# Attention's decay products ahead of the second head's projections, side blocks spread otherwise, RWKV state scaled behind the level mask

## The chip, the cores and the metric

One core of one Trainium2 chip runs the whole program. The metric is device time in microseconds (us) of one execution. The kernel before was run three times: 3910.09 us median, 3908.43 to 3912.69.

## The reference, cut to what matters

Two blocks over 512 tokens of width 1024, each of two layers, in float32. Block 1 per layer: modulated RMS norm, an RWKV-7 recurrence (8 heads of 64), a multiscale pooling, gates, output projection, gated feed-forward. Block 2 per layer: RMS norm, gated linear attention (GLA, 4 heads, key 128, value 256, both directions), grouped-query attention with rotary positions (8 heads), gates, feed-forward, and a gated per-layer embedding. What the change touches:

```python
# RWKV-7, per step
sk = einsum('bhvk,bhk->bhv', state, kk_t)
state = state * w_t - sk * (a_t * kk_t) + v_t * k_t
y_t = einsum('bhvk,bhk->bhv', state, r_t)
# GLA, per direction and head
la = log_sigmoid(ra @ w_alpha_up + b_alpha) / 16
cum = cumsum(la)                      # inside a chunk
q_dec, k_intra = q * exp(cum), k * exp(-cum)
# end of a layer of block 2
h = h + rms_norm(sigmoid(h @ w_ple_gate) * e, g_ple_post)
```

## The kernel before, in words

Five instruction streams are written out by hand and joined by semaphores: tensor, scalar, vector, gpsimd, sync. Activations lie feature-major, 128 features on the partitions and 512 tokens along the free axis. For float32 accuracy each operand is split into a high part (the round float32 format of the fast matmul) and a remainder, so each 128x128 weight block costs three matmuls of 512 columns (L420 to L422; L492 to L494 in side blocks; L815 to L817 in token-major products, where a product is 256 wide and each 128-token tile takes 24 of them).

Weights come as a stream of chunks of four blocks (256 KB), in exactly the order in which TensorE uses them, into a ring of 8 slots. The sync queue (SP) loads a chunk when TensorE has left the slot's last one (L2269); GpSimd makes the high part (L2245) and the remainder (L2247). The same queue carries the modulation columns (`ada_col`, 512 KB each, ring of three, L2263); the place of each is fixed by a list of chunk counts (`ada_at`), and a load is issued when the stream is 9 chunks past the place of the column three before it.

PSUM has 8 banks, dealt out in rotation by pool: "lin" banks 0 to 2, "lin2" 0 and 1, "bg2" 2 and 3, "bg" 3, "aux" 4 to 7. `begin` waits until the bank's last user has been read. `lane[0]` says which pool the projections take.

Where TensorE would wait for the other engines, it does side blocks: `side_jobs` names projections whose results are wanted only later (pool input and branch gates in block 1, 160 blocks a layer; one gate in each half of block 2, 64 blocks), and `fill(n)` does the next n of their blocks. ScalarE copies each finished gate to a staging tile and sends it to memory (`spill`, L1120 and L1123, in `gates_before`, with a wait for the spill before), and brings it back later (L1130, L1137). The constants at L57 to L63 say how many blocks stand where:

- `FILL_PREP` ahead of the RWKV chunks, `FILL_SCORE` behind each of the four score pairs of a chunk, `FILL_MEAN` (one number a layer) between mean and variance of each of four tiles, `FILL_POOL` ahead of the pool products; what is left is done behind the pool products, ahead of proj_a and proj_b.
- `FILL_CORE` ahead of each GLA head's core (four heads); inside a core 6 and 2 more; what is left is done behind head 3, ahead of the w_o_gla projections.

RWKV, `wkv_chunk`, four chunks of 128 tokens a layer: TensorE makes the scores of a pair of heads (L572, two banks) four times; VectorE multiplies each with the masks into `units` (L1861), then makes `mt` (L1866 twice, L1868); ScalarE copies the diagonal blocks into `ac`. TensorE starts the inversion (L586) when `mt` is there. VectorE makes the level masks 1 and 2 (L1873, in `level_part`), then goes through five levels with TensorE (L599, L611, L618; L1886), with one modulation column a level from the second on (L1666). Then w0, u, state and y. At the end of a chunk VectorE adds to the state `st` (L1903) and scales it (L1910); w0 and y of the next chunk read it.

GLA, `block2`: `group` makes ra, gq and gk of head 0; `gla_in` makes a head's gq, gk (for h > 0), values gv (token-major) and gates gg; `gla_decay` makes the decay logits of one head (two matmuls, L841), ScalarE takes Abs, Exp and Ln of them (L1368, L1372, L1375, two table loads), VectorE the sums (L1943 to L1966). Before, the order on TensorE is: decay 0, gv 0, decay 1, gg 0, gq 1, gk 1, decay 2, gv 1, decay 3, gg 1, core 0. `gla_factors` (ScalarE, L1386 to L1390) of head 0 waits for the sums of all four decays; `gla_keys` (VectorE, L1980 and L1983) makes qd and kd from them, for which the core's transposes (L853) wait. The core goes on with scores (L860), states (L870, L872), outputs (L884 to L888) and a norm (L895, L896); VectorE ends a head with `ot` (L2039, L2043) and its split into go_hi and go_lo (L1595, L1597), which the w_o_gla projections read.

The last norm of a block-2 layer: ScalarE squares the gated tiles (`square_gated`, L1439), TensorE sums them (L514), ScalarE takes the root (L1060).

## Time and profile before

| | |
|---|---|
| median of 3 runs | 3910.09 us |
| profiled execution, its own time | 3911.07 us |
| its span (first to last instruction) | 3909.2 us |
| mean granted TensorE clock | 0.975 |
| TensorE busy | 3731.4 us, 21300 matmuls |
| VectorE busy | 1806.1 us |
| ScalarE busy | 851.7 us |
| GpSimd busy | 2274.0 us |
| weight chunks | 1082, 256 KB each |

The profile is of one execution. Busy times of the engines overlap; the span is the time from the first to the last instruction, and the execution's own time is 1.9 us longer. A wait of an engine is idle time ahead of an instruction, put down to what ended it. Matmul durations in the timeline (0.39 us) are from start to end and overlap; the pace is read from the starts.

### The profile page before, as it was taken

The page shows a single profiled execution, that of the slowest core. Times are in us where ns is not written, and L with a number is a line of the kernel's source. Part 1 is how long each engine was busy: PE and PEld are TensorE (multiplying, and loading weights), DVE is VectorE, ACT ScalarE, POOL GpSimd, SP SyncE. Part 2 cuts the span into 40 slices and gives each one's busy share as a digit, 9 for nine tenths or more (in the row PEclk, how much of TensorE's full clock was granted, in tenths as well). Part 3 has the DMA queues.
Part 4 walks back from the last instruction along what each step waited for, and adds up shares of the span by engine and source line. Part 5 has one row for each costly group of instructions (what it writes and reads, how often), then busy time and mean ns, then how long its engine had stood idle before and what let it go on. Part 6 is the DMA issues. An engine that isn't in the chain of part 4 may idle for free.

```text
span 3909.2 us, 52952 instructions
## 1 busy us (share of the span) xinstructions
PE 3731.4 (95%) x21300; PEld 3022.7 (77%) x21300; DVE 1806.1 (46%) x2338; ACT 851.7 (22%) x1334; POOL 2274.0 (58%) x2218
## 2 busy tenths in 40 slices
PE   5999999999999899999899999999989999999997
PEld 4777678887777678887788677888777876778886
DVE  5643754234744653124443654523454435553235
ACT  3322110004222110003321532000243225220002
POOL 4512768776512767774556356777645463567773
PEclk9999999999999999998999999999989999999999
DMA  4223444342223443332223133333312231323332
GB/s 184 87 83 103 138 143 146 113 151 77 75 82 99 137 146 108 97 97 66 75 73 122 52 102 82 97 97 96 98 50 79 86 103 55 110 82 97 97 97 68
DMA packets 192195, 386.08 MB, mean 99 GB/s; under 512 B 21456, under 2 KB 21584, under 8 KB 190288
## 3 DMA queue, kind: packets, MB, share of 16 engines
q1 hardware_dynamic: 169776, 338.24, 29.1%
q10 hardware_dynamic: 22176, 44.45, 3.2%
q8 instruction: 170, 2.79, 0.3%
q14 instruction: 73, 0.60, 0.0%
HBM read 361.64 MB, written 20.97 MB: 98 GB/s over the span
## 4 chain that ended last, share of the span: by engine, by line
PE 86%; DVE 8%; ACT 4%; DMA 1%; issue 1%; ACTq 0%; SPq 0%; DVEq 0%
PE psum L420 18%; PE psum L421 18%; PE psum L422 18%; PE psum L492 3%; PE psum L494 3%; PE psum L493 3%; PE psum L514 2%; PE psum L981 1%; PE psum L956 1%; PE psum L599 1%; PE psum L611 1%; PE psum L467 1%; PE psum L468 1%; PE psum L469 1%; PE psum L618 1%; PE psum L572 1%
## 5 line engine op out<-in xcount | busy, mean ns | idle before, releaser
L2245 POOL TENSOR_SCALAR w_hi<-raw 128x512 fp32r<-128x512 f32 x1082 | 747.3, 691 | 1493.2 <-DMA raw<-weight_chunks 1489.5
L2247 POOL TENSOR_TENSOR w_lo<-raw,w_hi 128x512 fp32r<-128x512 f32 x1082 | 1491.1, 1378 | 90.3
L420 PE MATMUL psum<-in_hi,w_hi 128*128 128x512 f32 x1920 | 761.6, 397 | 3.8 <-ACT hs L1325 1.3
L421 PE MATMUL psum<-in_lo,w_hi 128*128 128x512 f32 x1920 | 749.3, 390 | 0.0
L422 PE MATMUL psum<-in_hi,w_lo 128*128 128x512 f32 x1920 | 748.8, 390 | 0.0
L420 PEld LDWEIGHTS psum<-in_hi,w_hi 128*128 128x128 f32 x1920 | 361.8, 188 | 91.7 <-issue 11.1
L421 PEld LDWEIGHTS psum<-in_lo,w_hi 128*128 128x128 f32 x1920 | 361.7, 188 | 79.8 <-issue 6.2
L422 PEld LDWEIGHTS psum<-in_hi,w_lo 128*128 128x128 f32 x1920 | 361.6, 188 | 75.7
L492 PE MATMUL psum<-in_hi,w_hi 128*128 128x512 f32 x576 | 255.0, 443 | 0.0
L494 PE MATMUL psum<-in_hi,w_lo 128*128 128x512 f32 x576 | 226.5, 393 | 0.0
L493 PE MATMUL psum<-in_lo,w_hi 128*128 128x512 f32 x576 | 226.4, 393 | 0.0
L1841 DVE TENSOR_TENSOR hs<-hs,psum 128x512 f32<-128x512 f32 x44 | 30.2, 687 | 295.5 <-PE psum L422 281.8
L2177 DVE TENSOR_TENSOR hs<-psum,rs_t 128x512 f32<-128x512 f32 x88 | 60.9, 691 | 228.5 <-PE psum L422 227.8
L1325 ACT ACTIVATE hs<-psum 128x512 f32<-128x512 f32 x44 | 26.3, 598 | 531.9 <-PE psum L422 531.8
L1666 DVE SCALAR_TENSOR_TENSOR ada_col<-ada_col,c_act 128x1024 f32<-128x1024 f32 x80 | 115.9, 1449 | 55.1 <-DMA ada_col<-ada_slabs 52.6
L492 PEld LDWEIGHTS psum<-in_hi,w_hi 128*128 128x128 f32 x576 | 108.6, 188 | 38.8 <-issue 17.3
L420 PE MATMUL psum<-hid_hi,w_hi 128*128 128x512 f32 x352 | 136.9, 389 | 0.0
L421 PE MATMUL psum<-hid_lo,w_hi 128*128 128x512 f32 x352 | 136.9, 389 | 0.0
L422 PE MATMUL psum<-hid_hi,w_lo 128*128 128x512 f32 x352 | 136.9, 389 | 0.0
L420 PE MATMUL psum<-h_hi,w_hi 128*128 128x512 f32 x352 | 136.9, 389 | 0.0
L421 PE MATMUL psum<-h_lo,w_hi 128*128 128x512 f32 x352 | 136.9, 389 | 0.0
L422 PE MATMUL psum<-h_hi,w_lo 128*128 128x512 f32 x352 | 136.9, 389 | 0.0
(427 smaller groups left out, 6700.4 us busy)
## 6 DMA issues: line engine op xcount, KB each, us to landing
raw<-weight_chunks SPq DMA_DIRECT2D x1082, 256.0 KB, 2.6
ada_col<-ada_slabs SPq DMA_DIRECT2D x80, 512.0 KB, 4.3
spill<-gate_st ACTq DMA_DIRECT2D x56, 256.0 KB, 2.7
ada_at<-ada_slabs SPq DMA_DIRECT2D x8, 1024.0 KB, 15.6
gin<-spill ACTq DMA_DIRECT2D x32, 256.0 KB, 3.4
mgs<-spill ACTq DMA_DIRECT2D x32, 256.0 KB, 3.0
sml<-small ACTq DMA_DIRECT2D x4, 1024.0 KB, 5.2
spill<-nt ACTq DMA_DIRECT2D x16, 256.0 KB, 2.6
```

The source lines that it names most:

```text
L420: pe.matmul(bank[:], wh, hi[:, i, :], start=(i == 0), stop=False)
L421: pe.matmul(bank[:], wh, lo[:, i, :], start=False, stop=False)
L422: ins = pe.matmul(bank[:], wl, hi[:, i, :], start=False, stop=(i == len(blocks) - 1))
L467: pe.matmul(bank[:], wh, in_hi[:, k, :], start=(k == 0), stop=False)
L492: pe.matmul(bank[:], wh, in_hi[:, k, :], start=(k == 0), stop=False)
L493: pe.matmul(bank[:], wh, in_lo[:, k, :], start=False, stop=False)
L494: ins = pe.matmul(bank[:], wl, in_hi[:, k, :], start=False, stop=(k == DT - 1))
L514: ins = pe.matmul(bank[:, t:t + 1], src[:, t * P:(t + 1) * P], kst[:, K_ONES, 0:1], start=(first and t == 0), stop=last, skip_group_check= ...
L1666: ins = stt(buf[:], buf[:], 1.0, c_act[:], ALU.mult, ALU.mult, accum_out=mods[l][:, m:m + 1])
L2177: tt(h[:, i, :], bank_of(job)[:], rs_t[:], ALU.mult).then_inc(bank_read(job), 1)
L2245: ts(w_hi[:, slot, :], raw[:, slot, :], 1.0, 1.0, ALU.mult, ALU.mult).then_inc(sem("chunk_hi"), 1)
L2247: ins = tt(w_lo[:, slot, :], raw[:, slot, :], w_hi[:, slot, :].bitcast(F32), ALU.subtract)
```

## The change

Five edits. The counts of side blocks in three constants. On both TensorE and ScalarE, the decays of block 2: decay 2 goes from behind head 1's gq and gk to ahead of them, and decay 3 from behind head 1's values to ahead of them. The pool of banks "lin2" is entered behind the first two heads' inputs instead of ahead of them. On ScalarE, the last of eight squares goes ahead of the activation that loads the Sqrt table. On VectorE, the state is scaled in the next chunk, between the masks of levels 1 and 2, instead of at the end of the chunk.

```diff
--- before.py
+++ after.py
@@ -57,10 +57,10 @@
 FILL_PREP = (8, 24)
 PE_BEFORE_SUM = 2
 PE_BEFORE_SPREAD = 4
-FILL_SCORE = (0, 2, 2, 4)
-FILL_MEAN = (16, 12)
+FILL_SCORE = (0, 2, 0, 5)
+FILL_MEAN = (16, 13)
 FILL_POOL = 8
-FILL_CORE = (8, 2, 2, 8)
+FILL_CORE = (5, 2, 2, 15)
 
 
 WINDOW_CHUNK = (8, 8, 10, 12)
@@ -819,15 +819,15 @@
                     ins.then_inc(done_sem(name + (t,)), 1)
                     close(name + (t,))
 
-            def gla_in(l, h, h_in, decays=()):
+            def gla_in(l, h, h_in, first=None, second=None):
                 if h:
                     projection(("gq", l, h), "w_in2", l, N_GQ + h, h_in)
                     projection(("gk", l, h), "w_in2", l, N_GK + h, h_in)
-                for d in decays[:-1]:
-                    gla_decay(l, d)
+                if first is not None:
+                    gla_decay(l, first)
                 token_major(("gv", l, h), l, "w_in2", N_GV + 2 * h)
-                for d in decays[-1:]:
-                    gla_decay(l, d)
+                if second is not None:
+                    gla_decay(l, second)
                 for j in range(2):
                     projection(("gg", l, h, j), "w_in2", l, N_GG + 2 * h + j, h_in)
 
@@ -924,9 +924,10 @@
                 group([(("ra", l), "w_in2", l, N_RA), (("gq", l, 0), "w_in2", l, N_GQ),
                        (("gk", l, 0), "w_in2", l, N_GK)], h_in)
                 side_jobs([(("g2a", l, m), "w_in2", l, N_GA + m) for m in range(DT)], "bg2")
+                gla_in(l, 0, h_in, 0, 1)
+                gla_decay(l, 2)
+                gla_in(l, 1, h_in, 3)
                 lane[0] = "lin2"
-                gla_in(l, 0, h_in, (0, 1))
-                gla_in(l, 1, h_in, (2, 3))
                 for h in range(GH):
                     gla_core(l, h)
                     if h + 2 < GH:
@@ -1333,7 +1334,7 @@
             norm_root(("nf", 0))
             squares(("m1", 0), ("rs", ("nf", 0)))
 
-            def gla_in(l, h, decays=()):
+            def gla_in(l, h, first=None, second=None):
                 if h >= 2:
                     act.wait_ge(sem("qd_ready"), count("qd_ready", (l, h - 2)))
                 for job, dst in ((("gq", l, h), gq[h % 2]), (("gk", l, h), gk[h % 2])):
@@ -1341,16 +1342,16 @@
                     act.wait_ge(*done(job))
                     af(dst[:], bank_of(job)[:], ACT.Copy).then_inc(bank_read(job), 1)
                     act.wait_ge(bank_read(job), turn(job))
-                for d in decays[:-1]:
-                    gla_decay(l, d)
+                if first is not None:
+                    gla_decay(l, first)
                 for t in range(NCH):
                     job = ("gv", l, h, t)
                     gates_before(job, gate_st2)
                     act.wait_ge(*done(job))
                     af(gv[h % 2][:, t, :], bank_of(job)[:, 0:GDV], ACT.Copy).then_inc(bank_read(job), 1)
                     act.wait_ge(bank_read(job), turn(job))
-                for d in decays[-1:]:
-                    gla_decay(l, d)
+                if second is not None:
+                    gla_decay(l, second)
                 if h >= 2:
                     act.wait_ge(sem("split_ready"), count("split_ready", ("go", l, 2 * (h - 2) + 1)))
                 for j in range(2):
@@ -1446,8 +1447,9 @@
                 act.wait_ge(*done(job))
                 af(ra[:], bank_of(job)[:], ACT.Copy).then_inc(bank_read(job), 1)
                 act.wait_ge(bank_read(job), turn(job))
-                gla_in(l, 0, (0, 1))
-                gla_in(l, 1, (2, 3))
+                gla_in(l, 0, 0, 1)
+                gla_decay(l, 2)
+                gla_in(l, 1, 3)
                 gla_factors(l, 0)
                 for h in range(GH):
                     gla_core(l, h)
@@ -1559,9 +1561,9 @@
                     act.wait_ge(bank_read(job), turn(job))
                     if m:
                         square_gated(l, m - 1)
+                square_gated(l, DT - 1)
                 af(warm[:], eps[:, 2:3], ACT.Sqrt).then_inc(sem("scalar_step"), 1)
                 act.wait_ge(sem("scalar_step"), passed("scalar_step"))
-                square_gated(l, DT - 1)
                 norm_root(("m5", l))
                 if l == 0:
                     squares(("m1", 1))
@@ -1875,6 +1877,10 @@
 
                 dve.wait_ge(sem("diag_ready"), count("diag_ready", (l, c)))
                 level_part(1)
+                if c:
+                    ins = tt(st[:], st[:], sscal[:, :, c - 1:c].to_broadcast([P, RT, P]), ALU.mult)
+                    ins.then_inc(sem("state_ready"), 1)
+                    dve.wait_ge(sem("state_ready"), passed("state_ready", (l, c)))
                 level_part(2)
                 for v in range(1, len(LEVELS)):
                     for name, t, second in (("mam", mi, 0), ("mamt", mt, 1)):
@@ -1907,9 +1913,6 @@
                         else:
                             ins.then_inc(sem("vector_step"), 1)
                             dve.wait_ge(sem("vector_step"), passed("vector_step"))
-                    ins = tt(st[:], st[:], sscal[:, :, c:c + 1].to_broadcast([P, RT, P]), ALU.mult)
-                    ins.then_inc(sem("state_ready"), 1)
-                    dve.wait_ge(sem("state_ready"), passed("state_ready", (l, c + 1)))
 
             def four(k):
```

## Rows read from the trace of the kernel before

**Rows 1.** Page, part 1: busy us, share of the span, instructions
```profile
PE 3731.4 (95%) x21300; PEld 3022.7 (77%) x21300; DVE 1806.1 (46%) x2338; ACT 851.7 (22%) x1334; POOL 2274.0 (58%) x2218
```

**Rows 2.** TensorE's waits: line, releaser, us in total, times, longest
```profile
PE psum L853 <- DVE kd L1983: 19.1, 2, 9.5
PE psum L586 <- DVE mt L1868: 17.0, 8, 2.2
PE psum L860 <- DVE ot L2039: 6.7, 2, 3.3
PE psum L815 <- ACT gv L1350: 5.7, 4, 1.4
PE psum L508 <- DVE yt L1792: 4.1, 3, 1.7
PE psum L514 <- ACT sqd L1439: 2.2, 2, 1.1
```

**Rows 3.** Timeline, TensorE, first w_o_gla projection: start, us, engine, line, operation
```profile
2064.78 0.39 PE L420 MATMUL psum<-go_hi,w_hi 128*128 128x512 f32 x1
2069.54 0.39 PE L420 MATMUL psum<-go_hi,w_hi 128*128 128x512 f32 x1
```

**Rows 4.** Timeline, VectorE, third chunk of layer 0; in brackets idle before, releaser
```profile
278.02 1.42 DVE L1861 TENSOR_TENSOR units<-psum,kst 128x512 f32<-128x512 f32 x2 [0.88 <-PE psum L572]
281.22 1.64 DVE L1868 TENSOR_TENSOR mt<-kst,mt 128x512 f32<-128x512 f32 x1
290.27 0.69 DVE L1873 TENSOR_TENSOR bm<-ac,kst 128x512 f32<-128x512 f32 x1
```

**Rows 5.** Timeline, GpSimd, the same chunk
```profile
279.57 1.08 POOL L2245 TENSOR_SCALAR w_hi<-raw 128x512 fp32r<-128x512 f32 x1 [9.77 <-DMA raw<-weight_chunks]
```

**Rows 6.** Windows: us; busy of five engines; granted clock; DMA share; GB/s
```profile
2039.00:2045.00 6.00, 6.00 (x29) 5.50 (x29) 5.08 (x10) 0.00 (x0) 0.00 (x0) 0.72 0.01 3
3093.00:3099.00 6.00, 6.00 (x26) 5.51 (x26) 4.27 (x8) 0.00 (x0) 0.00 (x0) 0.60 0.00 0
178.75:181.75 3.00, 3.00 (x37) 2.13 (x37) 1.65 (x2) 1.19 (x2) 2.21 (x2) 0.61 0.01 3
```

**Rows 7.** Timeline, VectorE, end of the same chunk
```profile
313.52 1.78 DVE L1666 SCALAR_TENSOR_TENSOR ada_col<-ada_col,c_act 128x1024 f32<-128x1024 f32 x1 [6.64 <-DMA ada_col<-ada_slabs]
322.50 0.88 DVE L1903 TENSOR_TENSOR st<-psum,st 64x256 f32<-64x256 f32 x2 [7.18 <-PE psum L690]
```

**Rows 8.** Page, part 6: DMA issues, KB each, median us to landing
```profile
spill<-gate_st ACTq DMA_DIRECT2D x56, 256.0 KB, 2.7
```

**Rows 9.** Timeline, ScalarE, linear attention of layer 0
```profile
1890.27 0.60 ACT L1360 ACTIVATE sg<-psum 128x512 f32<-128x512 f32 x1 [2.43 <-PE psum L422]
1896.62 1.28 ACT L1386 ACT_TABLE_LOAD   x1 [5.75 <-DVE dsc L1966]
```

**Rows 10.** Timeline, VectorE, the same stretch
```profile
1865.50 1.54 DVE L1943 TENSOR_SCALAR la<-psum,col 128x512 f32<-128x512 f32 x2 [6.55 <-ACT ln L1368]
1876.85 0.16 DVE L1966 TENSOR_TENSOR dsc<-dsc,la 128x3 f32<-128x3 f32 x1
1896.38 0.16 DVE L1966 TENSOR_TENSOR dsc<-dsc,la 128x3 f32<-128x3 f32 x1
1903.46 1.63 DVE L1983 TENSOR_TENSOR kd<-gk,ln 128x512 f32<-128x512 f32 x1
```

**Rows 11.** Timeline, VectorE, end of the fourth head
```profile
2067.38 1.66 DVE L1597 TENSOR_TENSOR go_lo<-ot,go_hi 128x512 fp32r<-128x512 f32 x1
```

**Rows 12.** Timeline, ScalarE, last norm of layer 1
```profile
3889.52 1.28 ACT L1562 ACT_TABLE_LOAD   x1
3891.05 0.63 ACT L1439 ACTIVATE sqd<-yy 128x512 f32<-128x512 f32 x1
3892.88 0.26 ACT L1060 ACTIVATE root<-psum,eps 128x4 f32<-128x4 f32 x1 [1.20 <-PE psum L514]
```

**Rows 13.** Timeline, VectorE, the same stretch
```profile
3888.94 0.69 DVE L2200 TENSOR_TENSOR yy<-mg,ee 128x512 f32<-128x512 f32 x1 [4.02 <-ACT mg L1558]
```

## The prediction

> **What bounds the kernel now.** The page's first part comes first: TensorE (PE) is busy 95% of the span [rows 1], so all that can be won without removing products is the 178 us in which it idles, plus what it loses at a lower clock. The list of PE's waits says where: 19.1 us before the transposes of the first attention head, 17.0 us before each chunk's inversion in the RWKV stage, 6.7 us before the scores of the fourth head, 5.7 us in the token-major value products, 4.1 us in the mean/variance stage of layer 1, 2.2 us before the last token sums [rows 2]. Each is short and repeated, so I go to the timeline around one of each and ask what ends it. The change touches six places; nearly everything in it is a move. A side block is three matmuls, started 0.68 us apart: eight blocks of one projection start between 2064.78 and 2069.54, seven steps in 4.76 us [rows 3]. The number of side blocks is fixed, so a block taken from one place is paid at another, and only idle time counts.
>
> **RWKV chunks (8).** Before: after scores d=2 PE does two side blocks, then scores d=3, then four. VectorE (DVE) sits idle 0.88 us before the last two mask products because of those two blocks (1.1 to 1.3 in the other seven chunks); the three steps behind them end with L1868, 1.64 us long, and only then may PE start the inversion [rows 4]. After: the two blocks go, so scores d=3 come 1.37 us earlier and the last pair of products follows the pair before it directly: 1.2 us earlier. PE has one block fewer to hide the rest (-0.68). That alone is 0.5 us a chunk. The larger part is L1868: an equal product from SBUF, L1873, takes 0.69 us when GpSimd (POOL) is idle [rows 4], and POOL's weight split began at 279.57, in the middle of this chain [rows 5]. The split comes 2.7 us after four blocks are used up, which now is 20 blocks = exactly five weight chunks per RWKV chunk, so it hits the same spot eight times. With 19 blocks the fourth one falls into the fill behind the scores, and the phase moves by one from chunk to chunk: I work out the split just behind L1868 in the first two chunks, on part of L1866 in the third, on L1868 in the fourth. Per layer the gain in idle is 1.5+1.7+1.2+0.6, in all about 9.5 us. Bounds: -5.5 us (nothing earlier, eight blocks less cover), 4.2 us (earlier scores only), 14.2 us (no split in any chain). PE's clock: after such a wait the granted clock is 0.61 over 3 us [rows 6], the 1.2 GHz level for most of it; 4 of the 8 stretches show a drop (0.61, 0.70, 0.75, 0.77), 1.2 to 1.6 us each. With waits of under 1 us most go: +4 us (0 to 6).
>
> **State scaled later** (L1910): DVE's 0.69 us leaves the head of the chain, but the scores of d=2 come behind PE's two blocks either way, so DVE only waits longer. Cost and gain 0; in its new place it delays the mask of level 2 by 0.7 us, which is used some 6 us later. If the cover went, 0.7 us a chunk.
>
> **The modulation products** hang on the same blocks: SP issues their load when the 16th block is done, DVE takes it at 313.52, and the state add comes at 322.50 [rows 7], 7.2 us of room behind it. With 19 blocks the release moves behind the cross and w0 steps, some 4 us: room 3 us, about 1 in the first chunk of a layer. I take 0.
>
> **Mean stage, layer 1:** +1 block in each of four turns. Three turns wait for yt, 4.1 us in all [rows 2], so three of the four blocks are covered: +2.0. Layer 0 keeps 16, so its four blocks fall behind the pool products. There they delay the last gate: its copy (0.60) and spill (2.7 us to land [rows 8]) now stand ahead of the gate loads on ScalarE's (ACT's) queue, and the whole proj_a/proj_b stretch follows those loads. 3.3 us later, 2.7 of it work: -0.6.
>
> **Linear attention (2 layers).** (a) Three banks in place of two for the first two heads: the third token tile needn't wait for ACT's copy of the first, which stands behind decay work. All 5.7 us [rows 2] go. (b) Head 0. Before: last gate copy ends 1890.87, but factors start at 1896.62, because [rows 9] the fourth decay's sums only end at 1896.54; keys ready 1905.09 [rows 10]. After: the third decay moves ahead of the second head's projections and the fourth ahead of the values. A decay beside values takes DVE 11.5 us, 1865.50 to 1877.01 [rows 10], and the fourth is then done near 1878. So the wait for the sums is gone, and the last gate copy is next: it comes 2.9 us earlier by (a), at 1888.0. Factors and keys take 8.5 us (1896.62 to 1905.09): ready at 1896.5. PE reaches the fill at 1887.3, waits 0.8 us for bank 2 (by the count of rotations the last gate product now lies in the side blocks' first bank, in both layers; hidden by the wait behind it), does 5 blocks (3.4), and waits to 1896.5: idle 5.8 instead of 9.5, +3.7 a layer, 7.4. Bounds 4 (keys slower by 1.7) and 12 (POOL quiet at the keys). (c) Head 3 gets 7 more blocks, 4.8 us, ahead of a wait of 3.3 a layer: +6.7, and the granted clock of 0.72 and 0.60 over 6 us behind it [rows 6] recovers: +1.7 and +2.4. (d) The price: 8 blocks instead of 12 remain between head 3 and w_o_gla, 2.7 us less. There the eighth block starts at 2069.54 [rows 3], and its input is ready at 2069.04 [rows 11]: 0.5 us of room. New wait 2.2 us a layer, and one of the two clocks drops: -5.6 (bounds -3 and -9). Moved instructions: two products per decay, and ACT's chain of six activations and two table loads, 6.8 us; the copies of gq and gk queue behind it, which PE doesn't wait for with three banks. Side blocks finish elsewhere, so gate copies (0.6 and a spill issue) shift on ACT; each falls where ACT waits for PE. Cost 0; if not, 0.9 us each.
>
> **Last square** ahead of the Sqrt table load, twice. ACT loads the table at 3889.52 and squares at 3891.05, root at 3892.88 [rows 12]; the input was ready at 3889.63 [rows 13]. After: square 3889.7, table and warm-up from 3890.35 to 3891.9 beside PE's sums (1.1 us), root at 3891.9: +1.0 each, 1.9. A rule speaks against it: the Trainium skill, ScalarE: Activation LUTs, section What ACT_TABLE_LOAD costs, gives 1283 ns for the load and 1380 ns of drain. The rows agree with the load's length and leave no room for the rest: load and warm-up together take 1.53 us, 3889.52 to 3891.05 [rows 12]. By the page's sum root would be later than now, 0.3 us each instead of 1.0 earlier.
>
> **Sum:** 9.5 + 4 + 2.0 - 0.6 + 5.7 + 7.4 + 6.7 + 4.1 - 5.6 + 1.9 = 35.1 us. From the profiled execution's own 3911.07 us (1 us over the median 3910.09): 3876.
>
> **Rivals.**
> 1. POOL's splits stay on the masks: the shift of one block moves them by 0.7 us or a fill, and products of 0.7 to 1.6 us are easily hit. Then the chunks give 4.2 and no clock: 35.1 - 9.3 = 25.8, 3885. The Trainium skill, SBUF — State Buffer, section Who interferes with whom, says such a DVE product is blocked for the rest of POOL's instruction; by that rule, [rows 4, 5] agree (1.64 against 0.69 us).
> 2. Attention gives back more: the longer fill of head 3 keeps POOL busy beside DVE's ot chain (1.5 us of wait left a layer, clock low again, -7), and (d) costs 3 more. 3886; with rival 1, 3895.
> 3. Slower: the modulation load. If the block that frees it falls behind the 19th, into the next chunk's first fill, DVE waits for it in front of the state add, and the masks behind that: release near 273.3, 5 us of load, 1.8 of product, 280.2 against a state add at 270.6, 9.6 us at each of six transitions, 58 us: 3876 + 58 = 3934. Against: my count gives blocks 16 and 17 in the phases that matter, inside the chunk.
> 4. It doesn't do what it says: only one decay really moves ahead of the projections, and if the factors are held by the gate copies as much as by the sums, while masks come no sooner (-5.5), gains and prices cancel: 3905 to 3910.
> 5. The table switch costs the page's drain: 3878.5.
>
> **Chances.** Forecast 0.60 (its own range 3866 to 3885), rival 1 0.20, rival 2 with or without 1 0.10, rival 5 0.02: all faster, 0.92. Rival 4: 0.03, taken as no change. Rival 3: 0.05. A measurement of this kernel tells about 0.2%, 8 us, from no change. The range 3861 to 3896: below, chunks at 14.2 and 6, head 0 at 12; above, rivals 1 and 2 together.
>
> **What would show it.** Waits of PE: kd near 10 us and a bank wait of 0.8 ahead of the fill, mt L1868's group (now line +4 or so) from 17 to under 9, ot and gv gone, yt near 2, a new wait for go_lo near 4.4; L1868's product near 0.7 us in about half the chunks; root 1 us sooner behind the last square. Wrong if the mt wait stays over 2 us a chunk, if kd stays over 15, or if the state add waits for an ada load.

## The result, and the profile after

The kernel after takes 3861.65 us (median of 4 runs, 3860.92 to 3868.89), the kernel before 3909.53 us beside it: ratio of after to before 0.9881, 95% interval 0.9868 to 0.9895, 47.9 us less. Forecast were 35.1 us less, 3876 us, with a range from 3861 to 3896: the right direction, but the median lies only 0.65 us above the lower edge of the range. The profiled execution of the kernel after is the slowest of its four, 3868.89 us, so that profile against profile the gain is 42.2 us.

The page of the kernel after, part 1 (busy us, share of the span, instructions), answers to [rows 1]:

```profile
PE 3717.1 (96%) x21300; PEld 3015.2 (78%) x21300; DVE 1797.5 (46%) x2338; ACT 851.8 (22%) x1334; POOL 2274.2 (59%) x2222
```

With the same 21300 matmuls TensorE is busy 14.3 us less and idle 27.9 us less (149.9 in place of 177.8): part of the gain is not idle time but TensorE's clock. TensorE's waits (line, releaser, us in total, times, longest) answer to [rows 2], and like them they are an excerpt; L586 waits for L1870 now, the old L1868:

```profile
PE psum L853 <- DVE kd L1986: 9.1, 2, 4.6
PE psum L586 <- DVE mt L1870: 8.4, 8, 1.7
PE psum L420 <- DVE go_lo L1599: 4.6, 2, 3.0
PE psum L508 <- DVE yt L1794: 1.8, 2, 1.1
PE psum L492 <- ACT sg L1361: 1.5, 2, 0.7
PE psum L514 <- ACT sqd L1440: 0.8, 1, 0.8
```

The waits for ot and gv are gone, kd and mt are halved, and two waits are new, go_lo and the bank held by sg. Forecast were 10, under 9, 4.4, near 2 and 1.6 for the first five. One longer wait is in neither excerpt, that of L420 for mt (L1818, behind proj_a and proj_b): 15.4 us before, 13.6 after, and between 10.3 and 15.4 in the fourteen profiles of this study.

**The masks of a chunk.** VectorE in the first and the third chunk of layer 0 (start, us, engine, line, operation), against [rows 4]:

```profile
174.61 1.41 DVE L1868 TENSOR_TENSOR mt<-units,kst 64x512 f32<-64x512 f32 x2
176.05 0.69 DVE L1870 TENSOR_TENSOR mt<-kst,mt 128x512 f32<-128x512 f32 x1
...
270.53 2.17 DVE L1868 TENSOR_TENSOR mt<-units,kst 64x512 f32<-64x512 f32 x2
272.74 0.69 DVE L1870 TENSOR_TENSOR mt<-kst,mt 128x512 f32<-128x512 f32 x1
```

GpSimd's split in the same two chunks, against [rows 5]:

```profile
176.65 0.62 POOL L2248 TENSOR_SCALAR w_hi<-raw 128x512 fp32r<-128x512 f32 x1 [4.61 <-DMA raw<-weight_chunks]
...
269.45 0.62 POOL L2248 TENSOR_SCALAR w_hi<-raw 128x512 fp32r<-128x512 f32 x1 [10.81 <-DMA raw<-weight_chunks]
```

In the first chunk the split starts 0.6 us after the last product began, and that product takes 0.69 us in place of 1.64. In the third it has moved forward onto the pair before it (2.17 in place of 1.41). The phase drifts as the prediction worked out, and PE's waits for mt follow it: 0.80, 0.80, 1.56, 1.15 in layer 0 and 0.79, 0.81, 1.66, 0.81 in layer 1, against 2.1 eight times before.

**The clock behind these waits.** Windows of 8 us that take in the wait or its end, second chunk of layer 0 (us; busy of five engines; granted clock; DMA share; GB/s), first before, then after:

```profile
228.00:236.00 8.00, 6.57 (x89) 5.13 (x89) 2.95 (x3) 1.20 (x2) 2.95 (x3) 0.79 0.13 35
```

```profile
220.00:228.00 8.00, 7.20 (x86) 5.37 (x87) 6.42 (x8) 3.06 (x5) 3.16 (x3) 1.00 0.18 66
```

Four of the eight chunks of before show 0.79 in such a window; none of after does. 0.21 of 8 us is 1.7 us each. The prediction had read it over 3 us only [rows 6] and so missed the rest of each spell at the 1.2 GHz level.

Another drop got longer. Layer 1's first scores stand behind a wait for bonus (L1783), 2.59 us before and 3.38 after, and at the start of that chunk (6 us, first before, then after) the clock reads:

```profile
1047.00:1053.00 6.00, 6.00 (x31) 4.39 (x31) 4.02 (x6) 1.20 (x2) 1.88 (x2) 0.77 0.33 124
```

```profile
1037.00:1043.00 6.00, 5.61 (x21) 4.25 (x22) 4.39 (x7) 1.20 (x2) 1.60 (x2) 0.50 0.27 101
```

From its first pair of scores to its third that chunk takes 1.3 us longer for it than before (6.14 against 4.88).

**Head 0**, layer 0, against [rows 9, 10]. ScalarE's last gate copy and the table load of the factors:

```profile
1868.86 0.60 ACT L1361 ACTIVATE sg<-psum 128x512 f32<-128x512 f32 x1 [3.56 <-PE psum L422]
1869.47 1.28 ACT L1387 ACT_TABLE_LOAD   x1
```

VectorE's last keys:

```profile
1876.13 1.63 DVE L1986 TENSOR_TENSOR kd<-gk,ln 128x512 f32<-128x512 f32 x1
```

TensorE's fill and the transposes behind it:

```profile
1869.51 0.50 PE L492 MATMUL psum<-in_hi,w_hi 128*128 128x512 f32 x1 [0.75 <-ACT sg L1361]
1877.82 1.54 PE L853 MATMUL psum<-kst,kd 128*128 128x128 f32 x6 [4.62 <-DVE kd L1986]
```

The table load of the factors follows the last gate copy directly; before, 5.75 us of waiting for the sums lay between. From its start to the end of the keys it is 8.3 us (forecast 8.5), and the bank wait is 0.75 (forecast 0.8).

**Last norm, layer 1**, ScalarE, against [rows 12]:

```profile
3848.84 0.63 ACT L1440 ACTIVATE sqd<-yy 128x512 f32<-128x512 f32 x1 [0.21 <-DVE yy L2203]
3849.49 1.28 ACT L1565 ACT_TABLE_LOAD   x1
3851.02 0.26 ACT L1061 ACTIVATE root<-psum,eps 128x4 f32<-128x4 f32 x1
```

The first token sum starts at 3847.09, root 3.93 us behind it; before, 4.92 (3887.96 to 3892.88). That is the 1.0 us forecast.

**The modulation load** (rival 3). VectorE at the change to the second chunk of layer 1, against [rows 7]:

```profile
1084.48 1.63 DVE L1668 SCALAR_TENSOR_TENSOR ada_col<-ada_col,c_act 128x1024 f32<-128x1024 f32 x1 [10.35 <-DMA ada_col<-ada_slabs]
...
1086.54 0.88 DVE L1909 TENSOR_TENSOR st<-psum,st 64x256 f32<-64x256 f32 x2 [0.42 <-PE psum L690]
```

The product now waits for its load until close ahead of the state add, but the add still waits for TensorE, not for the load. Of the room, 5.20 us at this change before, 0.42 us is left; at the later changes it is 2.8 and 12.3 us. In e6 to e9, e11 and e13 below nothing is left at the first change of layer 1, in some of them of layer 0 too: the add follows the product at once, and in e7 TensorE then waits 0.22 and 0.73 us for the state. So rival 3 does exist, on a small scale.

### The profile page after: what moved, and what is told of

It reads as the page before. It is cut to its first block, busy times and chain, and to the rows that moved or that the text cites. A ratio compares the mean times of both kernels' runs of the same rounds, so it can differ in the third digit from the quotient of the medians.

```text
span 3867.0 us, 52950 instructions
## 1 busy us (share of the span) xinstructions
PE 3717.1 (96%) x21300; PEld 3015.2 (78%) x21300; DVE 1797.5 (46%) x2338; ACT 851.8 (22%) x1334; POOL 2274.2 (59%) x2222
## 4 chain that ended last, share of the span: by engine, by line
PE 86%; DVE 9%; ACT 2%; DMA 1%; issue 1%; ACTq 0%; SPq 0%; DVEq 0%
PE psum L420 18%; PE psum L421 18%; PE psum L422 18%; PE psum L492 3%; PE psum L494 2%; PE psum L493 2%; PE psum L514 2%; PE psum L982 1%; PE psum L957 1%; PE psum L611 1%; PE psum L467 1%; PE psum L599 1%; PE psum L815 1%; PE psum L817 1%; PE psum L816 1%; PE psum L468 1%
## 5 line engine op out<-in xcount | busy, mean ns | idle before, releaser
L420 PE MATMUL psum<-in_hi,w_hi 128*128 128x512 f32 x1920 | 761.2, 396 | 2.9 <-ACT hs L1326 1.3
L420 PEld LDWEIGHTS psum<-in_hi,w_hi 128*128 128x128 f32 x1920 | 361.8, 188 | 90.7 <-issue 11.1
L1530 ACT ACTIVATE hs<-hs 128x512 f32<-128x512 f32 x44 | 27.8, 633 | 495.9 <-DVE hs L2180 495.9
L420 PE MATMUL psum<-hid_hi,w_hi 128*128 128x512 f32 x352 | 136.9, 389 | 0.0
L420 PE MATMUL psum<-h_hi,w_hi 128*128 128x512 f32 x352 | 136.9, 389 | 0.0
```

Of the source, the lines that this page charges most:

```text
L420: pe.matmul(bank[:], wh, hi[:, i, :], start=(i == 0), stop=False)
```

## The experiments

Experiments e1 to e4 take the change apart, each part alone on the kernel before (median beside them 3911.4 us of 19 runs). Theory A, of the prediction: waits and clock in the chunks, and waits in the linear attention, are two separate gains; the state's new place and the square are small. Its rivals were that the state's place carries the chunk gain, and that the parts share one gain.

**e1, blocks of the RWKV stage alone.**

```diff
-FILL_SCORE = (0, 2, 2, 4)
-FILL_MEAN = (16, 12)
+FILL_SCORE = (0, 2, 0, 5)
+FILL_MEAN = (16, 13)
```

> The kernel before with FILL_SCORE (0, 2, 0, 5) and FILL_MEAN (16, 13) alone. Theory A (scores come earlier, the weight split leaves the mask products, TensorE's clock no longer drops behind the chunk waits): 20 to 24 us faster than before; the eight mt waits fall from 17.0 to about 8.5 us in all and the granted clock in the 3 us behind each is 1.00. Theory B (the later state scaling carries part of it, because VectorE starts its masks 0.7 us sooner in six chunks): 14 to 19 us, mt waits of 10 us or more.

Measured: 3887.48 us, ratio 0.9939 (0.9922 to 0.9955), 23.9 us less. The wait for mt is 6.2 us, for kd 19.1 as before, and the clock over the 3 us behind each of the eight waits is 1.00. The constants carry the whole RWKV gain: the eight chunks take 391.0 us here, 393.2 in the kernel after and 416.2 before.

**e2, the state's place alone.**

```diff
                 level_part(1)
+                if c:
+                    ins = tt(st[:], st[:], sscal[:, :, c - 1:c].to_broadcast([P, RT, P]), ALU.mult)
...
-                    ins = tt(st[:], st[:], sscal[:, :, c:c + 1].to_broadcast([P, RT, P]), ALU.mult)
```

> The kernel before with the state scaled behind the mask of level 1 alone. Theory A: VectorE waits longer for the scores of d=2 and nothing else moves: within 1 us of before, mt waits 17 us. Theory B: 0.7 us at six chunk starts reach TensorE: 4 us faster, mt waits near 13 us.

Measured: 3909.56 us, ratio 0.9995 (0.9986 to 1.0004); mt 17.1. No effect that shows, as forecast.

**e3, linear attention alone** (on TensorE; ScalarE's order of the decays likewise).

```diff
-FILL_CORE = (8, 2, 2, 8)
+FILL_CORE = (5, 2, 2, 15)
...
+                gla_in(l, 0, h_in, 0, 1)
+                gla_decay(l, 2)
+                gla_in(l, 1, h_in, 3)
                 lane[0] = "lin2"
-                gla_in(l, 0, h_in, (0, 1))
-                gla_in(l, 1, h_in, (2, 3))
```

> The kernel before with the decay order, the banks and FILL_CORE (5, 2, 2, 15) of the changed kernel alone. Theory A: the linear attention stages are independent of the rest: 20 to 22 us faster, kd wait near 9 us, ot and gv waits gone, a new go_lo wait near 4.5 us. Theory B: part of what the attention stage showed came from the phase of the weight stream, shifted by the RWKV side blocks: 15 us or less.

Measured: 3889.33 us, ratio 0.9944 (0.9929 to 0.9959), 22.1 us less. kd 9.4, go_lo 5.6, sg 1.5; ot and gv gone; mt 17.2.

**e4, the last square alone.**

```diff
+                square_gated(l, DT - 1)
                 af(warm[:], eps[:, 2:3], ACT.Sqrt).then_inc(sem("scalar_step"), 1)
                 act.wait_ge(sem("scalar_step"), passed("scalar_step"))
-                square_gated(l, DT - 1)
```

> The kernel before with the last square ahead of the Sqrt table load alone. By the rows (load 1.28 us, next activation right behind it): 2 us faster, root 1.0 us sooner behind the start of the last token sums. By the page's drain: 0.6 us slower, root 0.3 us later.

Measured: 3908.85 us, ratio 1.0000 (0.9990 to 1.0009). The wait for sqd falls from 2.2 us to 0.8; in the time, where 2 us were expected, it is below what this measurement separates.

The product of the four ratios is 0.9878, the whole change has 0.9881: within their intervals the parts add up, and none hides another.

Experiments e5 to e8 vary the kernel after, one thing each (kernel before beside them: 3913.5 us).

**e5, twenty blocks a chunk; e6, nineteen but two of them ahead of scores d=3.** With before and after they make a table of order by count.

```diff
-FILL_SCORE = (0, 2, 0, 5)
-FILL_MEAN = (16, 13)
+FILL_SCORE = (0, 2, 0, 6)
+FILL_MEAN = (16, 12)
```

> The kernel after with FILL_SCORE (0,2,0,6) in place of (0,2,0,5) and FILL_MEAN (16,12) in place of (16,13): 20 side blocks a chunk again, but the scores of d=3 still without blocks ahead of them. Theory A (what counts is how late mt comes behind the scores, that is earlier scores plus POOL's split off the last product): five weight chunks a RWKV chunk put the split at the same spot eight times, the one it has in the first chunk of after, just behind the last mask product. One block more covers 0.68 us of the waits of 0.8 (and 1.6 in the third chunk goes to the same): the wait for mt falls from 8.4 us to under 2, eight times 0.1 to 0.2; the fill in the mean stage of layer 1 has one block fewer a turn, its wait for yt goes from 1.8 to about 4 us, and layer 0's left-over blocks behind the pool products vanish. In sum 4 to 6 us under the kernel after. Rival B (the phase must drift from chunk to chunk, or the split will lie on the masks, as in before): waits of 1.5 us a chunk, clock below 0.8 again behind them, 5 to 10 us over the kernel after.

```diff
-FILL_SCORE = (0, 2, 0, 5)
+FILL_SCORE = (0, 2, 2, 3)
```

> The kernel after with FILL_SCORE (0,2,2,3): the 19 blocks a chunk of after, but two of them still ahead of the scores of d=3. It tells the two halves of the chunk gain apart. Theory A1 (earlier scores carry it, POOL's phase is a side matter): waits for mt of 2.0 us or more in all eight chunks, as 1.2 us of VectorE's idle time returns, low clock behind about half of them, 15 to 20 us over the kernel after. Theory A2 (the split off the last product carries it): the split moves by one block a chunk, so two or three chunks of four have the last product at 0.7 us and waits near 1.8, the others over 2.8; 10 to 14 us over the kernel after.

Measured: e5 3862.02 us (3855.35 to 3867.77), ratio 0.9872 (0.9853 to 0.9891); e6 3882.15 us, ratio 0.9923 (0.9908 to 0.9937). PE's wait for mt, in us over eight chunks:

| | 20 blocks | 19 blocks |
|---|---|---|
| two blocks ahead of scores d=3 | 17.0 (before) | 16.8 (e6) |
| none ahead | 0 (e5) | 8.4 (after) |

e5 has no line for this wait at all; 0.1 us of idle time a chunk without a releaser stays. VectorE in its first chunk:

```profile
172.51 1.41 DVE L1868 TENSOR_TENSOR mt<-units,kst 64x512 f32<-64x512 f32 x2
173.95 0.69 DVE L1870 TENSOR_TENSOR mt<-kst,mt 128x512 f32<-128x512 f32 x1
174.67 2.71 DVE L1875 TENSOR_TENSOR bm<-ac,kst 128x512 f32<-128x512 f32 x2
```

GpSimd beside it:

```profile
174.54 0.62 POOL L2248 TENSOR_SCALAR w_hi<-raw 128x512 fp32r<-128x512 f32 x1 [4.96 <-DMA raw<-weight_chunks]
```

The split now starts 0.4 to 0.8 us after the product that TensorE waits for has begun, eight times out of eight; the product takes its 0.69 us, and the split falls on the level masks (2.71 us for two here), which nobody waits for. So the phase need not drift; it must only be the right one, and rival B falls. The table says more: with 20 blocks as before, moving the scores alone takes the whole wait away, and the count of 19 gives 8.4 us of it back. Yet eight blocks more in the chunks are 5.4 us of work for these 8.4 us, and the eight fronts (from the first score to the inversion) are only 1.9 us shorter than in after, 83.9 against 85.9. The rest of what was expected lay at the mean stage and behind the pool products. In the time, where 4 to 6 us less were expected, e5 can't be told from the kernel after.

In e6 the split moves through the chunks. VectorE in its second and fourth chunk of layer 0, where PE waits 1.55 and 2.53 us:

```profile
225.12 1.41 DVE L1868 TENSOR_TENSOR mt<-units,kst 64x512 f32<-64x512 f32 x2
226.56 0.69 DVE L1870 TENSOR_TENSOR mt<-kst,mt 128x512 f32<-128x512 f32 x1
...
326.60 2.36 DVE L1868 TENSOR_TENSOR mt<-units,kst 64x512 f32<-64x512 f32 x2
329.00 0.69 DVE L1870 TENSOR_TENSOR mt<-kst,mt 128x512 f32<-128x512 f32 x1
```

0.95 us more for the pair of products is 0.98 us of longer wait; in the first chunk of each layer it is the last product that is longer (1.64 us). Four of eight chunks wait 1.5 to 1.6 us, four 2.5 to 2.8: A2's pattern, and not A1's 2.0 or more in all eight. The time fits A1's 15 to 20 us better: 20.5 us over after by the medians (16 by the ratios), where A2 expected 10 to 14. Both halves count: the split's place moves a single wait by 1.0 us, but the sum over the eight, 16.8 us, is that of before, and it is the order that halves it. Of 15.3 us in the chunks of the two profiles, 12.6 are in the fronts (98.5 against 85.9), 2.7 behind them. The waits for mt make 8.4 of the 12.6; another part is the change between side blocks and scores itself. TensorE's last two pairs of scores in the third chunk of layer 0, before:

```profile
274.14 0.70 PE L572 MATMUL psum<-qr,b_f 64*128 64x256 f32 x4
274.67 0.60 PE L572 MATMUL psum<-qr,k_f 64*128 64x256 f32 x4
276.79 0.70 PE L572 MATMUL psum<-qr,b_f 64*128 64x256 f32 x4
```

And after:

```profile
266.40 0.70 PE L572 MATMUL psum<-qr,b_f 64*128 64x256 f32 x4
266.94 0.60 PE L572 MATMUL psum<-qr,k_f 64*128 64x256 f32 x4
267.37 0.60 PE L572 MATMUL psum<-qr,b_f 64*128 64x256 f32 x4
```

From pair to pair it is 2.65 us with the blocks and 0.97 without, 1.68 less, of which two blocks are 1.37: 0.31 us come on top of the work moved.

**e7, four blocks from heads 1 and 2 to head 0; e8, old order of the decays.**

```diff
-FILL_CORE = (5, 2, 2, 15)
+FILL_CORE = (9, 0, 0, 15)
```

> The kernel after with FILL_CORE (9,0,0,15): the two side blocks ahead of each of heads 1 and 2 go ahead of head 0, where TensorE still waits 4.6 us a layer for the keys. Theory: those four blocks hide nothing where they are (no wait stands there in after), and each hides 0.68 us in its new place: kd's wait falls from 9.1 to 3.7 us, 5.4 us under the kernel after. Rival: without them a wait appears at head 1 or 2 (qd or kd of these heads, or ot), which takes back 1 to 1.5 us at each of four places: no change.

```diff
                 gla_in(l, 0, h_in, 0, 1)
-                gla_decay(l, 2)
-                gla_in(l, 1, h_in, 3)
+                gla_in(l, 1, h_in, 2, 3)
```

(and the same on ScalarE)

> The kernel after with the order of the decays as before (0, values 0, 1, gates 0, gq 1, gk 1, 2, values 1, 3, gates 1), all else as after. Theory: the sums of the fourth decay end late again and hold ScalarE's factors; head 0 has now five blocks to cover it in place of eight, so kd's wait goes from 9.1 us to about 20: 9 to 13 us over the kernel after. Rival (the three banks alone free the chain, since the last gate copy comes as late as the sums): within 3 us of the kernel after.

Measured: e7 3850.10 us (3848.17 to 3851.79), ratio 0.9841 (0.9824 to 0.9857), 11.5 us under the kernel after (16 by the ratios); e8 3876.38 us, ratio 0.9909 (0.9894 to 0.9924), 14.7 over it (11 by the ratios; 9 to 13 expected). PE's waits of e7, then of e8:

```profile
PE psum L853 <- DVE kd L1986: 3.8, 2, 1.9
...
PE psum L420 <- DVE go_lo L1599: 1.0, 2, 0.5
```

```profile
PE psum L853 <- DVE kd L1984: 18.6, 2, 9.3
```

e8: without the new order the sums hold the factors again, and the wait for kd is as long as before. But the wait alone misleads, since TensorE reaches it at different times. Counted from the first decay product (L841) of layer 0, in us (layer 1 differs by some 0.2 at most):

| | last gate copy ends | last sums end | last kd ends | TensorE starts to wait |
|---|---|---|---|---|
| before (two banks, old order) | 64.93 | 70.61 | 79.16 | 69.68 |
| e8 (three banks, old order) | 61.56 | 67.22 | 74.53 | 65.31 |
| e9 (two banks, new order) | 64.90 | 53.61 | 73.25 | 67.61 |
| after (three banks, new order) | 61.55 | 52.08 | 69.86 | 65.30 |

So the third bank alone brings the keys 4.6 us forward and the new order another 4.7; the third bank's share doesn't show in the wait because TensorE comes 4.4 us earlier too (two of these for the three blocks fewer). Of the 4.6 us, 0.9 are one kd product that takes 0.69 us in e8 and 1.63 in before and after.

e7: kd is where it was expected (3.7), and no wait appears at heads 1 and 2. The surplus is the wait for go_lo, 4.6 to 1.0 us. It was not expected; VectorE's closing chain of head 3 in the kernel after, and in e7:

```profile
2034.03 1.40 DVE L1597 CAST go_hi<-ot 128x512 fp32r<-128x512 f32 x1
...
2036.98 1.58 DVE L2046 TENSOR_TENSOR ot<-ot,sg 128x512 f32<-128x512 f32 x1
...
2039.05 0.98 DVE L1599 TENSOR_TENSOR go_lo<-ot,go_hi 128x512 fp32r<-128x512 f32 x1
```

```profile
2023.45 0.43 DVE L1597 CAST go_hi<-ot 128x512 fp32r<-128x512 f32 x1
...
2025.71 0.88 DVE L2046 TENSOR_TENSOR ot<-ot,sg 128x512 f32<-128x512 f32 x1
...
2027.09 1.06 DVE L1599 TENSOR_TENSOR go_lo<-ot,go_hi 128x512 fp32r<-128x512 f32 x1
```

The same products, 10.9 us from reciprocal to end in one and 9.8 in the other; in layer 1 it is 12.2 and 9.9. These 1.1 and 2.4 us are nearly all of the 3.6 us of wait: GpSimd's splits again, in another phase. Behind the wait for kd the clock of 6 us is 0.72 and 1.00 in e7, where it is 0.60 and 0.56 in the kernel after: 3.4 us more.

**e9, two banks; e11, four blocks back behind head 3; e12 and e13, combinations** (kernel before beside these four: 3906.2 us, 7 us less than beside e5 to e8, so ratios say more than medians across the two groups).

```diff
+                lane[0] = "lin2"
                 gla_in(l, 0, h_in, 0, 1)
                 gla_decay(l, 2)
                 gla_in(l, 1, h_in, 3)
-                lane[0] = "lin2"
```

> The kernel after with the pool of banks lin2 entered ahead of the first two heads' inputs, as before; the decays stay in their new order. Theory: the values of heads 0 and 1 wait again for ScalarE's copy of the tile before the last, 5.7 us in the two layers as before, and the last gate copy comes 2.9 us later a layer; the wait of 1.5 us for a bank ahead of head 0 (copy of sg) goes. Since kd waits 9.1 us for a chain that starts at that copy, kd's wait shrinks by no more than what the values' waits push the fill back: time 4 to 8 us over the kernel after. Rival (the waits for gv went with the decays' order, not with the third bank): no wait for gv, within 2 us of the kernel after.

```diff
-FILL_CORE = (5, 2, 2, 15)
+FILL_CORE = (5, 2, 2, 11)
```

> The kernel after with FILL_CORE (5,2,2,11): four of the fifteen blocks ahead of head 3 stay for the place ahead of w_o_gla. It weighs the gain (c) against the price (d) of the prediction. Theory: 11 blocks cover three more than before's 8, 2.0 of the 3.3 us that head 3 waited for ot, so 1.3 us a layer return, 2.6 in all; the wait for go_lo, 4.6 us in the two layers, goes altogether: idle 2 us less than in after, and the clock decides: 0 to 4 us under the kernel after. Rival (the fill of 15 keeps GpSimd busy beside VectorE's ot, so fewer blocks make ot sooner): no wait for ot at all, 4 to 6 us under it.

```diff
-FILL_SCORE = (0, 2, 0, 5)
-FILL_MEAN = (16, 13)
-FILL_CORE = (5, 2, 2, 15)
+FILL_SCORE = (0, 2, 0, 6)
+FILL_MEAN = (16, 12)
+FILL_CORE = (9, 0, 0, 15)
```

> Two edits of earlier runs together: FILL_SCORE (0,2,0,6) with FILL_MEAN (16,12), and FILL_CORE (9,0,0,15). The second alone gave 3850.1 us, 11.5 under the kernel after; the first alone gave 3862.0, where its profile has no wait for mt at all, against 8.4 us, and where eight blocks more in the chunks (5.4 us) were saved at the mean stage and behind the pool products. Theory: the parts add up; the idle time worked out is 3 to 6 us less than with the second alone: 3844 to 3850. Rival (weight chunks in the same phase in every RWKV chunk cost elsewhere what the wait gives): 3850 to 3858.

```diff
-FILL_CORE = (5, 2, 2, 15)
+FILL_CORE = (9, 0, 0, 15)
...
                 level_part(1)
-                if c:
-                    ins = tt(st[:], st[:], sscal[:, :, c - 1:c].to_broadcast([P, RT, P]), ALU.mult)
...
+                    ins = tt(st[:], st[:], sscal[:, :, c:c + 1].to_broadcast([P, RT, P]), ALU.mult)
```

> FILL_CORE (9,0,0,15) as in e7, and the state scaled at the end of the chunk, as before. The first experiment (blocks alone, state at the end) showed 6.2 us of wait for mt in eight chunks, the kernel after 8.4 us. Theory (the state's place costs nothing): within 2 us of e7's 3850.1. Rival (its new place between the masks of the levels pushes mi and mt of the level steps, or moves weight chunks' phase, 0.3 us a chunk): 2 to 5 us under e7.

| | median us | ratio to before, 95% | wait kd | other waits, us |
|---|---|---|---|---|
| after | 3861.65 | 0.9868 to 0.9895 | 9.1 | mt 8.4, go_lo 4.6 |
| e9 | 3871.70 | 0.9902 to 0.9932 | 11.5 | gv 5.7, go_lo 4.5 |
| e11 | 3860.72 | 0.9871 to 0.9901 | 8.5 | ot 2.6, gs 1.6 |
| e7 | 3850.10 | 0.9824 to 0.9857 | 3.8 | mt 8.1, go_lo 1.0 |
| e12 | 3850.77 | 0.9841 to 0.9872 | 3.0 | yt 4.1, no mt |
| e13 | 3851.10 | 0.9846 to 0.9879 | 4.0 | mt 7.7 |

e9: 10 us over the kernel after (14 by the ratios), where 4 to 8 were expected. The 5.7 us for gv are back, and kd didn't shrink but grew by 2.4: the chain to the keys starts at the last gate copy, which two banks delay as well, by 3.4 us a layer. The third bank paid twice. In its profile the two attention stages are 6.2 us longer than in after, as expected; a stage that no edit touches (from layer 1's first norm sums, L514, to L508, ahead of its RWKV chunks) takes 101.6 against 95.5 us at a clock of 0.87 against 0.93, as it does in the profiles of e1 and e2, so part of the surplus may not be the edit's. e11: the trade of (c) and (d) comes out even in the time, 2.6 us of ot wait (as expected) against 4.6 of go_lo. e12: no mt wait, yet no gain over e7; in its profile TensorE idles 4.2 us less than in e7's (3850.0 - 3714.3 against 3849.9 - 3710.0) and is busy 4.3 us longer. The clock's scatter doesn't explain it: the mean granted clock is 0.980 in both. Whether it is a price of the constant phase, one profile of each doesn't tell; this stays open, and the time lies in the rival's range. e13: by the medians within 1 us of e7, as expected, by the ratios 9 us over it, with intervals that overlap: no worth of the state's place shows. e7, e12 and e13, 3850 to 3851 us, have lower medians than both kernels of the case; e7's interval alone lies wholly under that of the kernel after.

## Why the prediction was right, and where its sizes were off

Term by term, in the two profiled executions. For a chunk, "front" is from the first score to the start of the inversion, "rear" the rest; a minus is time saved.

| step of the prediction | forecast | measured |
|---|---|---|
| chunks, front: idle 9.5 and a block (0.68) fewer in each of eight | -14.9 | -16.5 |
| chunks, rear: clock | -4 | -6.5 |
| mean stage of layer 1: 4 blocks in, 2.0 covered | +0.7 | +0.5 |
| layer 0's left-over blocks | +3.3 | +2.4 |
| linear attention, both layers | -18.3 | -21.2 |
| last square | -1.9 | -1.0 in layer 1; -0.8 in layer 0, with a change of clock in it |

**Chunks.** The eight fronts sum to 102.4 us before and 85.9 after, the rears to 313.8 and 307.4. The rears hold the same work, and they differ by 1.6 us in exactly the four chunks whose window shows 0.79. What happens in the kernel after is as forecast: earlier scores, the split off the last product in most chunks, waits under 1 us in five of eight. Why it happens was half wrong. The prediction gave the scores' new place 4.2 us (its bound for "earlier scores only") and the larger part to the count of 19, which makes the phase drift. In e5, with 20 blocks and the new place alone, the split is off the product eight times out of eight and the wait is gone; in e6, with 19 and the old place, the wait is what it was. The order carries the gain, and the drift costs 8.4 us of it, for which the blocks taken out of the chunks pay back 5.4. That the sum came out near 9.5 is luck in this respect (and its four terms a layer, 1.5 + 1.7 + 1.2 + 0.6, make 10.0 in two layers).

In the front, 16.5 us are 8.6 of waits for mt (17.0 less 8.4; 9.5 forecast), 5.4 of blocks, and 2.5 that no step had: 0.4 to 0.6 us in each of seven chunks, the 0.31 us found with e6 among it, less 0.8 in the first chunk of layer 1, where the low clock behind the wait for bonus lasts longer. The step that was mis-sized most is "1.2 to 1.6 us each" for a spell of low clock: each is 1.7 us by windows of 8 us, four of them, 6.5 us against the 4 taken and the bound of 6. Rival 1 (splits stay on the masks) is refuted by the rows of both chunks above.

That such a product is held while GpSimd works agrees with the rule of the Trainium skill, SBUF — State Buffer, section Who interferes with whom, in the pairs here: 0.69 against 1.64, 0.43 against 1.40, 0.88 against 1.58 us (the 0.88 is itself held for a part; free it is 0.69). It holds the other way too. In the last chunk of layer 1 in the kernel after, the last product starts at 1195.58 and takes its 0.69 us; the split that starts just behind it is the longer one, 1.14 in place of 0.62 us:

```profile
1195.62 1.14 POOL L2248 TENSOR_SCALAR w_hi<-raw 128x512 fp32r<-128x512 f32 x1 [10.45 <-DMA raw<-weight_chunks]
```

**State scaled later: nothing that shows**, by e2 and e13.

**Attention.** (a) gv: all 5.7 us, as forecast, and e9 shows that the third bank does it, and brings the last gate copy forward as well, by 3.4 us a layer (2.9 forecast). (b) kd plus the new bank wait: 19.1 to 10.6, 8.5 us won against 7.4 forecast; e8 and e9 show that it takes both the order and the third bank, as the prediction had it: the order takes the sums out of the way, the bank brings the copy forward. (c) ot: all 6.7. (d) go_lo 4.6 against 4.4. The idle terms sum to 16.3 us (5.7 + 8.5 + 6.7 - 4.6); the stages, from the first decay to the first product (L508) of the grouped-query attention, are 11.2 and 10.0 us shorter, so 4.9 us more, of which the prediction had 4.1 - 1.2 as clock; the other 2.0 have no term. The clock behind head 3 and behind go_lo went as forecast. Windows of 6 us behind the go_lo waits of both layers, and behind head 3's transposes, in the kernel after:

```profile
3082.90:3088.90 6.00, 6.00 (x20) 4.76 (x21) 0.69 (x1) 2.55 (x3) 1.90 (x2) 0.72 0.42 125
2040.20:2046.20 6.00, 6.00 (x27) 4.96 (x28) 0.69 (x1) 2.55 (x3) 3.38 (x4) 1.00 0.56 189
3051.70:3057.70 6.00, 6.00 (x41) 5.53 (x40) 5.76 (x8) 1.80 (x3) 4.10 (x4) 1.00 0.28 87
2011.20:2017.20 6.00, 6.00 (x41) 5.55 (x40) 5.73 (x8) 1.80 (x3) 3.38 (x4) 1.00 0.25 87
```

Both drops behind head 3 [rows 6] are gone and one has come behind go_lo, in layer 1. Rival 2 (attention gives back more) is refuted: no ot wait, and no higher price at (d).

**Last square.** Load and warm-up take 1.53 us here too (3849.49 to 3851.02). The Trainium skill, ScalarE: Activation LUTs, section What ACT_TABLE_LOAD costs, adds 1380 ns of drain to the load; no row has room for it, and rival 5 falls. Rival 3 didn't occur in this kernel, though the room in layer 1 shrank to 0.4 us (about 1 was worked out), and in e7 it is used up. Rival 4 is refuted by e1 and e3.

**The rest of the miss.** The forecast was 7.1 us above the profiled execution: 1.6 + 2.5 in the chunks and 2.9 in the attention make 7.0, and what is left in the small terms and in the stages that no edit touches nearly cancels. The other 7.2 us are between that execution and the median of its kernel, and have no term. One stage shows where such time can go: the pool products to the next norm in layer 0 take 106.2 us in this profile at a clock of 0.95, but 101.4 to 105.0 in those of the seven others whose side blocks there are the same (e1, e6 to e9, e11, e13). The other three executions of the kernel after left no trace, so this is an indication, not shown.

## What to carry to other kernels

Filler work is free only where the thing waited for doesn't stand behind it: two blocks ahead of the last scores looked like cover and cost 16 to 20 us in eight chunks. Where GpSimd's work makes VectorE's products longer (0.69 to 1.64 us here), count the filler in whole weight chunks and see where in the period the split falls: behind the product that the bound engine waits for, it costs no wait (e5), and if the period repeats exactly, that holds every time. Whether the time follows has to be measured; e5 is no faster than the kernel after. Read a wait together with the moment at which the bound engine gets there: in e8 it stayed at 18.6 us although the keys came 4.6 us a layer sooner. Rank the places of filler by the wait behind each: e7 is one line of constants, moves blocks from where no wait stands, and wins a quarter (by the ratios a third) as much again as the whole change.

## What the runs showed of the hardware that was not expected

**The short spells of low clock cost the same each.** One window over a stage of the second block's layer 1 that no edit touches (between two norms, 1500 matmuls, no wait of TensorE in it), before and then after; columns as in the windows above:

```profile
3486.67:3824.66 337.99, 337.99 (x1500) 280.28 (x1499) 116.34 (x137) 22.62 (x35) 243.31 (x245) 0.99 0.33 96
```

```profile
3447.53:3783.95 336.42, 336.42 (x1499) 279.06 (x1498) 118.99 (x137) 22.61 (x35) 244.62 (x245) 1.00 0.33 96
```

1.6 us apart, the same as between the rears of chunks. The same profiles have longer spells too (0.50 over 6 us above). The length of 338 us shows up in this stage in 5 of the 14 profiles of this study, whatever the edit, so a gain of 2 us can't be read off the length of one stage of one profile. The 6.1 us of e9 above warn of the same on a larger scale.

**A longer wait doesn't decide it alone.** e6 waits 2.53 us ahead of the inversion in the fourth chunk of layer 0 and 2.78 in the first. The windows of 8 us behind them:

```profile
178.40:186.40 8.00, 7.93 (x139) 6.64 (x141) 1.76 (x3) 1.79 (x3) 1.47 (x2) 0.80 0.18 68
...
329.80:337.80 8.00, 7.96 (x171) 6.80 (x172) 4.77 (x6) 1.98 (x4) 2.31 (x2) 1.00 0.10 35
```

In before, waits of 2.09 to 2.15 us were followed by 0.79 in four chunks and by 1.00 in the other four. In the nine kernels with the scores moved up, after and e12 among them, no such wait is over 1.80 us, and one alone, that of 1.80 in e8, has a spell behind it. Shorter waits removed the spells nearly every time; what picks one wait of 2.1 us and not the next, these runs don't say. At the wait for bonus ahead of layer 1's first chunk the length does tell: over the 6 us behind it the clock is 0.75 to 0.77 in the five profiles with waits of 2.55 to 2.75 us, and 0.50 to 0.56 in the nine with waits of 2.99 to 3.57 us.
